# An input projection of 88 column tiles: 60 of them as 30 pairs of seven block products, with weight sums formed on the chip

## The chip, the cores and the metric

The kernel runs on one core of a Trainium2 chip. The metric is the device time of one execution in microseconds (us), the median of repeated runs. Engines are named as the profile names them: PE is TensorE's matmul and PEld its weight load, DVE is VectorE, ACT is ScalarE, POOL is GpSimd, SP is SyncE, which here issues most of the loads.

## What is computed

One layer of a hybrid backbone over 640 tokens (128 of context, 512 latent) of width 2048. Only its front matters here: a modulation vector from the conditioning, a normalised and modulated input `h`, and the combined input projection of 11,312 columns.

```python
mod = (cond @ p['w_mod'][l] + p['b_mod'][l])[:, None, :]
shift1, scale1, gate1, shift2, scale2, gate2 = jnp.split(mod, N_MOD, axis=-1)
h = rmsnorm(x, p['pre1_gain'][l]) * (1 + scale1) + shift1
...
proj = h @ p['w_in'][l] + p['b_in'][l]
(dq, dk, dv, dz, db, da, mq, mk, mv, mo, mi, mf, ga, gb) = split_columns(proj)
```

Two recurrent branches, their merge, and sixteen experts follow; the change doesn't touch them. All values are float32.

## The kernel before

All of the front is in `phase_front` (L163). The projection is cut into 88 column tiles of 128 columns and a gate tile of 48 (tile number 88). The result of a tile is 128 channels by 640 tokens, in two PSUM banks of 320 tokens each (`CHUNKS`), and it sums over 16 slices of 128 inputs. For float32 accuracy, each operand is split into a rounded high part and a low rest, and a product is taken as high x high + high x low + low x high. So a tile is 16 x 3 x 2 = 96 matmuls of 320 columns, in `products` (L288), called by `project` (L303).

The stages of a tile run on different engines. SP loads its weights (1 MB, from `d_win`) into a ring of four slots (L231 to L239). ACT makes the high half (`high`, L410), DVE the low half (`low`, L539), each two tiles ahead, and PE waits for `win_low`. After the matmuls ACT evicts the two banks with the bias (L476 to L486), and POOL stores the 320 KB of the tile (L255). Tiles 0 to 23 get a convolution instead, on DVE and ACT; tiles 24 to 39 are evicted in column-major token order; tiles 40 to 87 as they are.

Between the tiles runs the modulation product: 96 chunks of 128 inputs (1 MB each, from `d_wmod`), four matmuls of 512 columns each, in the four column strips of the array, so that they run side by side (`mod_products`, L265; the compiler makes two passes of each). Chunks 0 to 31 come before the projection; of the other 64 one comes before each tile from 24 on. Sixteen chunks are a group, which sums in one bank. At its end ACT copies the sums out (`copy_mod`, L393), PE turns them (`turn_mod`, L275), and DVE adds the bias (`store_mod`, L514). ACT issues the copy behind the last but one tile of a group (L489), and PE has a whole tile to do before it needs it.

The order of the loads is fixed by `mod_place` and `win_place` (L153 to L160). PE's program has loops over tiles 1 to 16 and over tiles 24 to 87 (L345); the programs of the other engines are written out. Behind the gate tile PE turns the gates (L361 to L366), DVE copies them, and the phase ends.

## Time and profile before

| | |
|---|---|
| median of 3 runs | 3760.63 us (3759.98 to 3760.92) |
| the profiled execution | 3755.26 us, of which the span from first to last instruction is 3753.4 us |
| PE busy | 3444.1 us, 92% of the span |
| DVE busy | 1960.6 us, 52% |
| ACT busy | 1663.3 us, 44% |
| POOL busy | 305.3 us, 8% |
| mean granted clock of TensorE | 0.959 of full speed |
| matmuls of L292 (the projection) | 8544, the first at 110.7 us, the last at 1466.9 us |

Matmuls are pipelined: the duration of one matmul in the trace is longer than its distance to the next one, so costs are taken from distances of starts. The idle time of an engine that waits for the one that is the bound costs nothing. "Granted clock" is the share of full speed that the chip allows TensorE; a mean of a stretch lies between its two levels, 0.5 (1.2 GHz) and 1.0 (2.4 GHz).

### The profile page before, as it was taken

The numbers are of one execution on the slowest core, as the hardware profiler recorded it, in microseconds if no ns is written. First come the engines' busy times: TensorE is split into PE (matmuls) and PEld (weight loads), VectorE is DVE, ScalarE is ACT, GpSimd is POOL, SyncE is SP. The second block draws the span as 40 slices with busy tenths as digits, with TensorE's granted clock in tenths as the row PEclk, the third lists the DMA queues.
The fourth block names the chain that finished last, engine by engine and source line by source line (L and its number), as shares of the span: only waits on it lengthen the run. The fifth ranks groups of instructions, "written<-read, shape, count | busy, mean of one in ns | idle before, by whom it ended". The sixth has DMA issues, their size and how long they took to land. (4 is left out here: it accounts for less than half of the span.)

```text
span 3753.4 us, 49971 instructions
## 1 busy us (share of the span) xinstructions
PE 3444.1 (92%) x20467; PEld 2846.4 (76%) x20467; DVE 1960.6 (52%) x2072; ACT 1663.3 (44%) x2033; POOL 305.3 (8%) x320
## 2 busy tenths in 40 slices
PE   5999999999999996999774899995999999999994
PEld 0899999999999996898753898875666666666663
DVE  1577411111111111545568434265888888888886
ACT  2445222211111112555432323343777777777774
POOL 0000000000000001332200100000001001010001
PEclk8999999999999998999986999996999999999997
DMA  9322344444444442112132533375999999999997
GB/s 410 135 91 89 107 157 156 159 157 161 158 166 162 156 156 80 48 34 67 42 91 68 194 121 127 134 292 223 360 399 385 391 399 376 400 391 382 398 378 293
DMA packets 172483, 796.85 MB, mean 212 GB/s; under 512 B 16532, under 2 KB 74132, under 8 KB 85284
## 3 DMA queue, kind: packets, MB, share of 16 engines
q1 hardware_dynamic: 154132, 701.71, 49.2%
q0 software_dynamic: 17328, 87.63, 7.0%
q10 hardware_dynamic: 864, 5.27, 0.3%
q8 instruction: 114, 1.87, 0.2%
q14 instruction: 45, 0.37, 0.0%
HBM read 732.10 MB, written 62.46 MB: 212 GB/s over the span
## 5 line engine op out<-in xcount | busy, mean ns | idle before, releaser
L2071 DVE TENSOR_TENSOR expert_lo<-expert_ring,expert_hi 128x2048 fp32r<-128x2048 f32 x384 | 879.4, 2291 | 159.6 <-ACT expert_hi L2008 156.5
L2008 ACT ACTIVATE expert_hi<-expert_ring 128x2048 fp32r<-128x2048 f32 x384 | 735.8, 1917 | 251.7 <-PE bank L1955 228.9
L292 PE MATMUL bank<-h_hi,win_hi 128*128 128x320 f32 x2848 | 656.1, 311 | 0.0
L292 PE MATMUL bank<-h_lo,win_hi 128*128 128x320 f32 x2848 | 647.1, 308 | 0.0
L292 PE MATMUL bank<-h_hi,win_lo 128*128 128x320 f32 x2848 | 646.9, 308 | 0.0
L541 DVE TENSOR_TENSOR win_lo<-front_ring,win_hi 128x2048 fp32r<-128x2048 f32 x89 | 203.8, 2290 | 821.3 <-ACT win_hi L414 821.3
L292 PEld LDWEIGHTS bank<-h_hi,win_hi 128*128 128x128 f32 x2848 | 473.1, 188 | 55.3 <-issue 55.3
L292 PEld LDWEIGHTS bank<-h_lo,win_hi 128*128 128x128 f32 x2848 | 476.4, 188 | 0.0
L292 PEld LDWEIGHTS bank<-h_hi,win_lo 128*128 128x128 f32 x2848 | 476.3, 188 | 0.0
L1953 PE MATMUL bank<-expert_hi,xeT_hi 128*80 128x512 f32 x1024 | 404.0, 395 | 1.2 <-DVE xeT_lo L2076 1.2
L1954 PE MATMUL bank<-expert_lo,xeT_hi 128*80 128x512 f32 x1024 | 402.3, 393 | 0.0
L1955 PE MATMUL bank<-expert_hi,xeT_lo 128*80 128x512 f32 x1024 | 398.9, 390 | 0.0
L485 ACT ACTIVATE x_tok<-bank,chan 128x320 f32<-128x320 f32 x96 | 45.3, 523 | 598.4 <-PE bank L292 598.4
L1576 ACT ACTIVATE merge_w_hi<-merge_ring 128x2048 fp32r<-128x2048 f32 x48 | 92.0, 1916 | 308.3 <-PE bank L1502 161.2
L1955 PEld LDWEIGHTS bank<-expert_hi,xeT_lo 128*80 128x80 f32 x1024 | 151.8, 148 | 85.8 <-issue 0.7
L1953 PEld LDWEIGHTS bank<-expert_hi,xeT_hi 128*80 128x80 f32 x1024 | 151.4, 148 | 84.8 <-issue 2.2
L1954 PEld LDWEIGHTS bank<-expert_lo,xeT_hi 128*80 128x80 f32 x1024 | 151.6, 148 | 81.0 <-issue 0.7
L1953 PE MATMUL bank<-expert_hi,hiddenT_hi 128*80 128x512 f32 x512 | 204.1, 399 | 0.0
L1954 PE MATMUL bank<-expert_lo,hiddenT_hi 128*80 128x512 f32 x512 | 200.9, 392 | 0.0
L1955 PE MATMUL bank<-expert_hi,hiddenT_lo 128*80 128x512 f32 x512 | 200.3, 391 | 0.0
L1668 DVE TENSOR_TENSOR merge_w_lo<-merge_ring,merge_w_hi 128x2048 fp32r<-128x2048 f32 x48 | 110.0, 2292 | 127.2 <-ACT merge_w_hi L1576 125.8
L414 ACT ACTIVATE win_hi<-front_ring 128x2048 fp32r<-128x2048 f32 x89 | 171.2, 1924 | 2.6 <-DMA front_ring<-d_win 2.6
(336 smaller groups left out, 4701.4 us busy)
## 6 DMA issues: line engine op xcount, KB each, us to landing
expert_ring<-d_wgate SPq DMA_DIRECT2D x128, 1024.0 KB, 7.2
expert_ring<-d_wup_e SPq DMA_DIRECT2D x128, 1024.0 KB, 7.8
expert_ring<-d_wdown SPq DMA_DIRECT2D x128, 1024.0 KB, 10.4
front_ring<-d_wmod SPq DMA_DIRECT2D x96, 1024.0 KB, 7.1
front_ring<-d_win SPq DMA_DIRECT2D x89, 1024.0 KB, 4.9
merge_ring<-d_wout SPq DMA_DIRECT2D x32, 1024.0 KB, 5.0
d_proj<-x_tok POOLq DMA_DIRECT2D x88, 320.0 KB, 2.5
merge_ring<-d_wup SPq DMA_DIRECT2D x16, 1024.0 KB, 5.0
```

Of the source, the lines that this page charges most:

```text
L292: mm = pe.matmul(bank[b][c][:, 0:hi - lo], wt[:, kk, :], h[:, kk, lo:hi], start=(kk == 0 and wt is w_hi[b] and h is k.h_hi), stop=(kk == K ...
L414: act.activation(w_hi[n % 2][:].rearrange("p k n -> p (k n)"), ring[place % FRONT_SLOTS][:], ACT.Copy).then_inc(s["win_high"], 1)
L485: ev = act.activation(ob[b][:, lo:hi], bank[b][c][:, 0:hi - lo], ACT.Identity, bias=bias(n))
L541: dve.tensor_tensor(w_lo[n % 2][:].rearrange("p k n -> p (k n)"), ring[win_place(n) % FRONT_SLOTS][:], w_hi[n % 2][:].rearrange("p k n -> ...
L1576: act.activation(w_hi[n % 2][:], w[:, n % 2], ACT.Copy).then_inc(s["w_high"], 1)
L1668: dve.tensor_tensor(w_lo[n % 2][:], w[:, n % 2], w_hi[n % 2][:].bitcast(F32), ALU.subtract).then_inc(s["w_low"], 1)
L1953: pe.matmul(out[0:CAP, :], a_hi, hi, start=first, stop=False)
L1954: pe.matmul(out[0:CAP, :], a_hi, lo, start=False, stop=False)
L1955: return pe.matmul(out[0:CAP, :], a_lo, hi, start=False, stop=last)
L2008: act.activation(w_hi[n % NSPLIT][:], w[:, n % NSLOT].rearrange("p (k n) -> p k n", n=HALF), ACT.Copy).then_inc(s["we_high"], 1)
L2071: dve.tensor_tensor(w_lo[n % NSPLIT][:], w[:, n % NSLOT].rearrange("p (k n) -> p k n", n=HALF), w_hi[n % NSPLIT][:].bitcast(F32), ALU.subt ...
```

## The change

Tiles 28 to 87 are taken in 30 pairs. A pair's weights are a 2 x 2 grid of blocks: the tile (first or second of the pair) by the half of the inputs (eight slices of 128). The tokens are a 2 x 2 grid too: half of the tokens (320) by half of the inputs. In place of the eight block products of the two tiles, seven are taken (Strassen's form with Winograd's order of sums), named by their weights: B11, T3, T1, T2, B21, T4, B22. T1 to T4 are sums of weight blocks, made by DVE for every pair. S1 to S4 are sums of the token blocks, made by DVE once (S1 to S3 during tiles 26 to 28, S4 in pair 0). Every sum is split into high and low halves like a plain operand. A block product is 8 x 3 = 24 matmuls of 320 columns into one bank. ACT and DVE put the products together into the four output blocks.

The order is now: tiles 0 to 23, the gate tile, tiles 24 to 27 (29 "classic" tiles in all), then the pairs. The modulation chunks 32 to 35 come at the classic places 21 to 24; the last 60 come as 120 halves of 512 KB through one buffer (`mod_half`), four per pair: after B11, T1, B21 and B22. Weights of the pairs come in quarters of 512 KB, each reloaded as soon as its product is done. High halves have three slots. `copy_mod` of a group comes in the pair after its last half, behind that pair's B11. PE's second loop is gone. The gates are turned behind tile 24 (the classic place 25); the vectors of the modulation are turned at the end. `h` and its halves keep their size but are laid out by token half.

The diff, cut to its core, in the order SP, PE, ACT, DVE, data layout (inner lines are moved to the left; output branches for the column-major tiles are left out):

```diff
+    def load_part(p, j, sem):
+        tile, half = PAIR_TILE + 2 * p + (j in (T3, B22)), (j in (B21, B22))
+        sp.dma_start(part(p, j)[:], k.d_win[tile][:, HALF_K * half:HALF_K * (half + 1), :]
+                     ).then_inc(s[sem], 16)
+    def load_mod_half(u):
+        if u < 4 * N_PAIRS:
+            wait(sp, s["half_used"], u)
+            q, h = half_of(u)
+            sp.dma_start(mod_half[:], k.d_wmod[q][:, 1024 * h:1024 * (h + 1)]).then_inc(s["half_in"], 16)
...
+    sp.wait_ge(s["s_low"], 3)
+    load_part(0, B21, "b21_in")
+    sp.wait_ge(s["proj_summed"], N_CLASSIC)
+    load_mod_half(0)
+    for p in range(N_PAIRS):
+        for j, sem in ((B11, "b11_in"), (T3, "b12_in"), (T1, "b22_in"), (B21, "b21_in")):
+            if p + 1 < N_PAIRS:
+                sp.wait_ge(s["part_summed"], part_number(p, j) + 1)
+                load_part(p + 1, B22 if j == T1 else j, sem)
+            if j != T3:
+                load_mod_half(4 * p + 1 + (B11, T1, B21).index(j))
+        load_mod_half(4 * p + 4)
 @block.gpsimd
...
+    def mod_half_chunk(u):
+        q, h = half_of(u)
+        g, kk = divmod(q, KT)
+        pe.wait_ge(s["half_in"], 16 * (u + 1))
+        if kk == 0 and h == 0:
+            pe.wait_ge(s["mod_copied"], g)
+        for j in range(4):
+            mm = pe.matmul(mod_sum(g)[32 * j:32 * j + 2, 256 * h:256 * (h + 1)], cond[:, kk, :],
+                           mod_half[:, 256 * j:256 * (j + 1)], start=(kk == 0 and h == 0),
+                           stop=(kk == KT - 1 and h == 1))
+        mm.then_inc(s["half_used"], 1)
...
+    def part_products(p, j):
+        m = part_number(p, j)
+        pe.wait_ge(s["part_low"], m + 1)
+        hi, lo = part_hi[m % HI_SLOTS], part_lo(p, j)
+        left_hi, left_lo = left[j]
+        for kk in range(HALF_K):
+            for x, (w, a) in enumerate(((hi[:, kk, :], left_hi), (hi[:, kk, :], left_lo),
+                                        (lo[:, kk, :], left_hi))):
+                mm = pe.matmul(part_bank[j][:, 0:HALF_T], w, a[:, kk, :],
+                               start=(kk == 0 and x == 0),
+                               stop=(kk == HALF_K - 1 and x == 2))
+        mm.then_inc(s["part_summed"], 1)
...
+    for p in range(N_PAIRS):
+        if p == 0:
+            pe.wait_ge(s["evac"], N_CLASSIC + 1)
...
+            pe.wait_ge(s["out_made"], MADE * p - 2)
+        part_products(p, B11)
+        mod_half_chunk(4 * p)
+        if p == 0:
...
+        else:
+            pe.wait_ge(s["out_made"], MADE * p - 1)
+        part_products(p, T3)
+        if p == 0:
...
+        else:
+            pe.wait_ge(s["out_made"], MADE * p)
+        part_products(p, T1)
+        mod_half_chunk(4 * p + 1)
+        part_products(p, T2)
...
+            turn_mod(GROUP_END[p - 1])
+        pe.wait_ge(s["p1_copied"], p + 1)
+        part_products(p, B21)
+        mod_half_chunk(4 * p + 2)
+        pe.wait_ge(s["out_made"], MADE * p + 2)
+        part_products(p, T4)
...
+            pe.wait_ge(s["s_low"], 4)
+        part_products(p, B22)
...
     def copy_mod(g):
-        act.wait_ge(s["mod_used"], KT * (g + 1))
+        if g < 2:
+            act.wait_ge(s["mod_used"], KT * (g + 1))
+        else:
+            act.wait_ge(s["half_used"], last_half(g))
...
+    def part_high(p, j):
+        m = part_number(p, j)
+        if m >= HI_SLOTS:
+            act.wait_ge(s["part_summed"], m - HI_SLOTS + 1)
+        if j in (B11, B21, B22):
+            act.wait_ge(s[{B11: "b11_in", B21: "b21_in", B22: "b22_in"}[j]], 16 * (p + 1))
+        else:
+            act.wait_ge(s["t_sum"], 4 * p + 1 + (T1, T3, T2, T4).index(j))
+        act.activation(part_hi[m % HI_SLOTS][:], part(p, j)[:], ACT.Copy).then_inc(s["part_high"], 1)
...
+    for p in range(N_PAIRS):
+        na = PAIR_TILE + 2 * p
+        act.wait_ge(s["part_summed"], part_number(p, B11) + 1)
+        wait(act, s["out_made"], MADE * p)
+        act.activation(u2[:], bank_a[:, 0:HALF_T], ACT.Copy)
+        wait_store(act, na)
+        if na < T_MLQ + PERM_TILES:
...
+        else:
+            act.activation(ob[0][:, 0:HALF_T], bank_a[:, 0:HALF_T], ACT.Identity, bias=bias(na)
...
+        for j in range(7):
+            m = part_number(p, j) + HI_SLOTS
+            if m < 7 * N_PAIRS:
+                part_high(*divmod(m, 7))
...
+            if j == B11 and p - 1 in GROUP_END:
+                copy_mod(GROUP_END[p - 1])
+    copy_mod(MOD_GROUPS - 1)
     act.wait_ge(s["rowp_in"], 16)
...
+    def t_sum(p, j):
+        out = part(p, j)[:]
+        if j == T1:
+            dve.wait_ge(s["b12_in"], 16 * (p + 1))
+            dve.wait_ge(s["b11_in"], 16 * (p + 1))
+            combine(out, b12[:], b11[:], ALU.subtract).then_inc(s["t_sum"], 1)
...
+    def split_low(m):
+        if m < 7 * N_PAIRS:
+            dve.wait_ge(s["part_high"], m + 1)
+            dve.tensor_tensor(part_lo(*divmod(m, 7))[:], part(*divmod(m, 7))[:],
+                              full(part_hi[m % HI_SLOTS][:]), ALU.subtract
+                              ).then_inc(s["part_low"], 1)
...
+    low(T_MLQ + 2)
+    dve.wait_ge(s["gates_turned"], 1)
+    dve.tensor_copy(k.gates[:], k.bank[6][:, 0:TT * 48].rearrange("p (t n) -> p t n", t=TT)
+                    ).then_inc(s["gates_copied"], 1)
...
+    combine(s1, full(a_hi[1][0]), full(a_hi[1][1]), ALU.add)
+    combine(s1, s1, full(a_lo[1][0]), ALU.add)
+    combine(s1, s1, full(a_lo[1][1]), ALU.add).then_inc(s["s_sum"], 1)
+    combine(s2, s1, full(a_hi[0][0]), ALU.subtract)
+    combine(s2, s2, full(a_lo[0][0]), ALU.subtract).then_inc(s["s_sum"], 1)
+    low(T_MLQ + 3)
+    s_low(0, s1_lo[:], s1_hi[:], s1)
...
+    low(T_MLQ + 4)
+    s_low(1, s2_lo[:], s2_hi[:], s2)
...
+    s_low(2, s3_lo[:], s3_hi[:], s3_sum[:])
...
+    for j in (T1, T3, T2):
+        t_sum(0, j)
+    split_low(0)
+    split_low(1)
+    t_sum(0, T4)
+    split_low(2)
...
+        split_low(part_number(p, B11) + HI_SLOTS)
+        if p == 0:
+            combine(s4_sum, full(a_hi[0][1]), full(s2_hi[:]), ALU.subtract)
+        split_low(part_number(p, T3) + HI_SLOTS)
+        if p == 0:
+            combine(s4_sum, s4_sum, full(s2_lo[:]), ALU.subtract)
+            combine(s4_sum, s4_sum, full(a_lo[0][1]), ALU.add).then_inc(s["s_sum"], 1)
+        split_low(part_number(p, T1) + HI_SLOTS)
+        dve.wait_ge(s["part_summed"], part_number(p, T2) + 1)
+        dve.wait_ge(s["p1_copied"], p + 1)
+        dve.tensor_tensor(u2[:], u2[:], bank_b[:, 0:HALF_T], ALU.add)
+        dve.drain().then_inc(s["out_made"], 1)
+        dve.tensor_tensor(u3[:], u2[:], bank_c[:, 0:HALF_T], ALU.add)
+        dve.drain().then_inc(s["out_made"], 1)
...
+        dve.drain()
+        dve.tensor_tensor(u2[:], u2[:], bank_d[:, 0:HALF_T], ALU.add)
+        dve.drain().then_inc(s["out_made"], 1)
+        if nxt:
+            t_sum(p + 1, T1)
+            t_sum(p + 1, T3)
+        if p == 0:
+            s_low(3, s4_lo, s4_hi, s4_sum)
+        split_low(part_number(p, T2) + HI_SLOTS)
+        if p - 1 in GROUP_END:
+            store_mod(GROUP_END[p - 1])
+        dve.wait_ge(s["part_summed"], part_number(p, B21) + 1)
...
+        else:
+            made = dve.tensor_tensor(ob[0][:, 0:HALF_T], ob[0][:, 0:HALF_T], bank_a[:, 0:HALF_T], ALU.add)
+        made.then_inc(s["out_made"], 1)
+        split_low(part_number(p, B21) + HI_SLOTS)
+        dve.wait_ge(s["part_summed"], part_number(p, T4) + 1)
...
+        else:
+            made = add_out(ob[0][:, HALF_T:T], bank_c[:, 0:HALF_T], bias(na), u3[:])
+        made.then_inc(s["out_made"], 1)
+        if nxt:
+            t_sum(p + 1, T2)
+        split_low(part_number(p, T4) + HI_SLOTS)
+        dve.wait_ge(s["part_summed"], part_number(p, B22) + 1)
+        if turned:
...
+        else:
+            made = add_out(ob[1][:, 0:HALF_T], bank_d[:, 0:HALF_T], bias(nb), u2[:])
+        made.then_inc(s["out_made"], 1)
+        if nxt:
+            t_sum(p + 1, T4)
+        split_low(part_number(p, B22) + HI_SLOTS)
     store_mod(MOD_GROUPS - 1)
...
-    whole = w.reshape(KT, P, MOD_GROUPS, D)[:, :, 2:].transpose(2, 0, 1, 3)
+    whole = w.reshape(KT, P, MOD_GROUPS, 4, 2, 256)[:, :, 2:].transpose(2, 0, 1, 4, 3, 5)
```

## Rows read from the trace of the kernel before

**Rows 1.** busy in one stretch: us, PE, PEld, DVE, ACT, POOL; clock, DMA share, GB/s

```profile
471.74:1467.28 995.54, 991.57 (x6769) 924.24 (x6761) 151.93 (x80) 193.68 (x228) 35.10 (x65) 1.00 0.40 153
```

**Rows 2.** timeline, ACT: start, us, engine, line, op; tiles 22, 23, 86, 87, gate

```profile
457.29 0.37 ACT L421 ACTIVATE x_tok<-bank,chan 128x128 f32<-128x128 f32 x1 [7.62 <-PE bank L292]
...
471.37 0.37 ACT L421 ACTIVATE x_tok<-bank,chan 128x128 f32<-128x128 f32 x1 [7.60 <-PE bank L292]
...
1437.52 0.94 ACT L485 ACTIVATE x_tok<-bank,chan 128x320 f32<-128x320 f32 x2 [12.51 <-PE bank L292]
...
1452.77 0.95 ACT L485 ACTIVATE x_tok<-bank,chan 128x320 f32<-128x320 f32 x2 [10.24 <-PE bank L292]
...
1467.28 0.36 ACT L493 ACTIVATE x_tok<-bank,chan 48x128 f32<-48x128 f32 x1 [13.57 <-PE bank L292]
```

**Rows 3.** timeline, PE, two matmuls in the expert stage

```profile
2622.89 0.39 PE L1953 MATMUL bank<-expert_hi,xeT_hi 128*80 128x512 f32 x1
2623.12 0.39 PE L1954 MATMUL bank<-expert_lo,xeT_hi 128*80 128x512 f32 x1
```

**Rows 4.** groups of instructions, 800 to 1400 us: busy, mean ns, idle before

```profile
L541 DVE TENSOR_TENSOR win_lo<-front_ring,win_hi 128x2048 fp32r<-128x2048 f32 x39 | 89.4, 2292 | 508.8 <-ACT win_hi L414 508.8
L414 ACT ACTIVATE win_hi<-front_ring 128x2048 fp32r<-128x2048 f32 x39 | 74.5, 1911 | 0.0
L267 PE MATMUL bank<-front_ring,cond 128*2 128x512 f32 x312 | 40.6, 592 | 2.6 <-issue 2.6
L485 ACT ACTIVATE x_tok<-bank,chan 128x320 f32<-128x320 f32 x78 | 36.8, 523 | 486.7 <-PE bank L292 486.7
...
L397 ACT ACTIVATE mod_rows<-bank 2x512 f32<-2x512 f32 x8 | 4.7, 586 | 0.1
...
L277 PE MATMUL bank<-const,mod_rows 128*128 128x128 f32 x8 | 1.2, 272 | 0.0
```

**Rows 5.** the same view, 130 to 370 us, one group of VectorE

```profile
L563 DVE TENSOR_TENSOR x_tok<-x_tok 128x640 f32<-128x640 f32 x16 | 13.1, 818 | 0.0
```

**Rows 6.** timeline, PE, one modulation chunk between two tiles

```profile
778.05 1.04 PE L267 MATMUL bank<-front_ring,cond 128*2 128x512 f32 x8
```

**Rows 7.** DMA, 800 to 1400 us: a queue; issues, KB each, median us to landing

```profile
q8 instruction: 36, 0.59, 0.4%
...
front_ring<-d_win SPq DMA_DIRECT2D x39, 1024.0 KB, 4.9
front_ring<-d_wmod SPq DMA_DIRECT2D x39, 1024.0 KB, 7.0
d_proj<-x_tok POOLq DMA_DIRECT2D x39, 320.0 KB, 2.4
```

**Rows 8.** the same view at 1841 us, one load

```profile
Cs<-d_smc SPq DMA_DIRECT2D x1, 512.0 KB, 3.8
```

**Rows 9.** timeline, PE, merge stage: four waits, idle time in brackets

```profile
2305.89 0.77 PE L1522 MATMUL bank<-merge_w_hi,yA_hi 128*128 128x512 f32 x1 [3.43 <-DVE yA_lo L1673]
...
2457.72 0.50 PE L1522 MATMUL bank<-merge_w_hi,yB_hi 128*128 128x512 f32 x1 [1.93 <-DVE merge_w_lo L1668]
...
2500.89 0.50 PE L1522 MATMUL bank<-merge_w_hi,yB_hi 128*128 128x512 f32 x1 [3.19 <-DVE merge_w_lo L1668]
...
2532.06 0.50 PE L1522 MATMUL bank<-merge_w_hi,yB_hi 128*128 128x512 f32 x1 [3.68 <-DVE merge_w_lo L1668]
```

**Rows 10.** PE by stretch, the microseconds behind those waits: busy, clock, DMA

```profile
2305.89:2313.89 8.00, 8.00 (x23) 0.64 0.90 346
2457.72:2465.72 8.00, 8.00 (x28) 0.79 0.95 356
2500.89:2508.89 8.00, 8.00 (x35) 1.00 0.63 204
2532.06:2539.00 6.94, 6.94 (x23) 0.75 0.49 151
```

**Rows 11.** timeline, DVE, the last instruction of the stage

```profile
1470.16 0.41 DVE L614 COPY gates<-bank 128x240 f32<-128x240 f32 x1 [2.48 <-PE bank L364]
```

More of the change, by code:

```diff
@@ L150, with tile_of, front_loads, part_number @@
 N_MOD_LOADS = MOD_GROUPS * KT
-def mod_place(q):
-    return q if q < 28 else q + 2 if q < 2 * KT else 58 + 2 * (q - 2 * KT)
-def win_place(n):
-    return 28 + n if n < 2 else 32 + n if n < T_MLQ + 2 else 59 + 2 * (n - T_MLQ - 2)
+HALF_T, HALF_K = T // 2, KT // 2
+N_CLASSIC = 29
+PAIR_TILE = 28
+N_PAIRS = (N_TILES - PAIR_TILE) // 2
+EARLY_MODS = 2 * KT + 4
+B11, T3, T1, T2, B21, T4, B22 = range(7)
+HI_SLOTS = 3
+MADE = 7
+def tile_of(o):
+    return o if o < T_MLQ else GATE_TILE if o == T_MLQ else o - 1
+def front_loads():
+    loads = [("mod", q) for q in range(28)] + [("win", o) for o in range(2)]
+    loads += [("mod", q) for q in range(28, 2 * KT)]
+    for o in range(2, N_CLASSIC):
+        if 23 <= o < 27:
+            loads.append(("mod", 2 * KT + o - 23))
+        loads.append(("win", o))
+    return loads
+FRONT_LOADS = front_loads()
+FRONT_PLACE = {load: place for place, load in enumerate(FRONT_LOADS)}
+def part_number(p, j):
+    return 7 * p + j
 def phase_front(nc, k):
+    def overlay(stack, specs):
+        return [stack.enter_context(nc.sbuf_tensor(n, shape, dt)) for n, shape, dt in specs]
+    QUARTER = [P, HALF_K, P]
+    TOKENS = [P, HALF_K, HALF_T]
     with ExitStack() as mem:
@@ new lines, in phase_front @@
+        with ExitStack() as between:
+            overlay(between, [("s3_front", [P, D], F32)])
+            s3_sum, = overlay(between, [("s3_sum", TOKENS, F32)])
+        PARTS = ("x0", "x1", "x2", "x3", "b21", "b12", "b11")
+        with ExitStack() as between:
+            sums = overlay(between, [(f"part_{n}", QUARTER, F32) for n in PARTS])
+        lows = overlay(mem, [(f"part_lo_{n}", QUARTER, F32R) for n in PARTS])
+        s3_lo, s3_hi = overlay(mem, [(n, TOKENS, F32R) for n in ("s3_lo", "s3_hi")])
@@ new lines, in phase_front @@
+        ob = overlay(mem, [(f"out_rows{b}", [P, T], F32) for b in range(2)])
+        w_hi, w_lo = (w_hi0, w_hi1), (w_lo0, w_lo1)
+        a_hi, a_lo = ([[h[:, r, HALF_K * c:HALF_K * (c + 1), :] for c in range(2)] for r in range(2)]
+                      for h in (k.h_hi, k.h_lo))
+        s4_hi, s4_lo = a_hi[1][0], a_lo[1][0]
+        s4_sum = k.h_lo_sum[:, 1, 0:HALF_K, :]
+        left = {B11: (a_hi[0][0], a_lo[0][0]), T3: (s3_hi[:], s3_lo[:]), T1: (s1_hi[:], s1_lo[:]),
+                T2: (s2_hi[:], s2_lo[:]), B21: (a_hi[0][1], a_lo[0][1]), T4: (a_hi[1][1], a_lo[1][1]),
+                B22: (s4_hi, s4_lo)}
@@ L179, in phase_front, with part_place, part, part_lo @@
+        place_of = {B22: 0, T1: 1, T2: 2, T4: 3}
+        def part_place(p, j):
+            return {B21: 4, T3: 5, B11: 6}[j] if j in (B21, T3, B11) else (place_of[j] + p) % 4
+        def part(p, j):
+            return sums[part_place(p, j)]
+        def part_lo(p, j):
+            return lows[part_place(p, j)]
+        b21, b12, b11 = sums[4:]
         RAW = T + 8
@@ L208, in phase_front @@
         x_sample, x_prompt = k.bank[4:6], k.bank[6:8]
-        N_PLAIN = N_TILES - T_MLQ
+        bank_a, bank_c, bank_d, bank_b = k.bank[2], k.bank[3], k.bank[0], k.bank[1]
+        part_bank = {B11: bank_a, T3: bank_c, T1: bank_d, T2: bank_b, B21: bank_a, T4: bank_c, B22: bank_d}
         def mod_sum(g):
```

279 lines of the change are left out of this document (190 added, 89 removed).

## The prediction

> **What bounds the kernel now.** I first read the busy time by stretch for the stage that the change touches, from the last tile of the convolved kind to the gate tile [rows 1]: TensorE is busy 991.57 of 995.54 us at a granted clock of 1.00, VectorE 151.93, ScalarE 193.68, and the DMA engines hold a share of 0.40. The stage ends when TensorE has issued its matmuls. The timeline of ScalarE then gives the cost of a tile, since its first eviction starts as the tile's last matmul ends [rows 2]. Tiles 22 to 23 are 471.37 - 457.29 = 14.08 us apart: 96 matmuls of 320 columns, 0.1467 us each. Tiles 86 to 87 are 15.25 apart: 1.17 us for one chunk of the modulation product between them. From tile 87 to the gate tile it is 14.51: 0.43 for four transposes. Tiles 17 to 23 are already written out without a loop, so straight-line code feeds TensorE at this pace; in the stage's loop 36 instruction fetches stand in 600 us [rows 7]. Of the stage, from 471.37 to the last gates copy at 1470.57 [rows 2, 11], 999.2 us are to be compared.
>
> **Taken away.** Sixty tiles were 60 x 8 half-by-half block products of 24 matmuls for 30 pairs of 16; now each pair has 7 block products over all 24 matmuls of 320 columns, where it had 8. A block is 24 x 0.1467 = 3.52 us, so a pair takes 24.64 where its two tiles took 28.16, and 30 pairs save 105.6 us. Both operand shapes stay. New is that 24 matmuls in a row add into one bank, where two banks took turns. In the expert stage three in a row add into one bank at 0.22 to 0.23 us for 512 columns [rows 3]: 0.213 of that is streaming at 2.4 GHz, the rest 0.01 to 0.02. The 320 columns stream in 0.133 of 0.1467, the same rest, so I take no loss.
>
> **The modulation chunks.** Of 96 chunks 60 now come as 120 halves, each a 512 KB load and 256 columns per matmul. A chunk's eight matmuls start in two waves of four: 1.04 us in all, 592 ns each [rows 4, 6]. A matmul of this type takes 592 ns at 512 columns and 272 at 128, so 0.833 ns per column and 379 at 256. Two waves each lose 0.213: 1.17 - 0.43 = 0.74 per half. Bounds are 0.585 (half a chunk) and 1.17 (no less than a whole). 120 x 0.74 = 88.8 against 60 x 1.17 = 70.2: a loss of 18.6. The four early chunks issued as 16 pieces stay at 1.17 each; if their halves serialise this adds up to 8 us, which I leave to the range.
>
> **New work beside TensorE.** Per pair VectorE gets eleven passes of 1024 elements and seven of 320. From 818 ns at 640 and 2292 at 2048 elements [rows 4, 5] they are 1.22 and 0.49 us: 13.4 + 3.4, with drains some 17.5 us in a pair of 27.6. ScalarE gets seven conversions of 1.1 (from 1911 at 2048) and two copies of 0.52: 8.7. Neither is the bound. What could bite is the order. Walking one steady pair from its first matmul: B11 ends at 3.5, T3 7.8, T1 11.3, T2 15.6, B21 19.1, T4 23.3, B22 26.9. The tightest step is the low half of B22: VectorE can start its four output sums at 15.6, then two weight sums, then this subtraction, ending at 21.8; TensorE wants it at 23.3. A third weight buffer and 7 us between release and use cover the others by 3 us and more. If VectorE took 25% longer, B22 would be the late one.
>
> **One-time waits.** Before tile 27's products VectorE has, from the gates' transposes on, a copy, five sums of 2560 elements (2.85 each) and then the 2.29 us split: 17 us, while TensorE has one tile of 14.08: 3.2 us idle. At the first pair the conversion is queued behind the last tile's eviction in three pieces (an estimate of 1.3, from 0.52 for 320 columns): 1.3 + 1.1 + 1.22, with handovers 3.7 us idle. In pair 0 three more sums of 2.85 and a subtraction stand ahead of B22: 3.4 us. Sum 10.3.
>
> **The copy at a group's end.** At pairs 6, 14 and 22 the half chunk behind B11 opens a new group and waits until ScalarE has copied the old one out. ScalarE gets there only after B11: copies 0.52 + 0.52, a conversion 1.1, then four copies of 0.586: with handovers 4.6 us, in which all of T3 to B22 is queued behind on TensorE. Before, this copy ran behind a whole tile. 3 x 4.6 = 13.8.
>
> **The load with the least cover.** There is one buffer for halves. Three of a pair's four loads have two blocks, 7.0 us; the one issued after B22's half is wanted after B11 alone, 3.52 us later, with SP free. Durations on SP are 4.9 us for 1 MB with the next megabyte 2.5 behind it (7.0 + 0.37 - 4.9), and 2.4 for a 320 KB store [rows 7]; the one undisturbed 512 KB load took 3.8 [rows 8]. Interpolating the first two gives 3.1, halving the megabyte 3.7. I take 3.8, the row of its own size: 3.8 + 0.1 - 3.52 = 0.4 us per pair, 26 pairs (the other three are under the copy): 10.4. Bounds: 0 at 3.1; 1.2 if the 320 KB store of the pair's second tile, issued in the same moment, goes first (0.31 of a megabyte, 0.77 us).
> The Trainium skill (DMA: Bandwidth & Descriptors, section Anatomy of one DMA) fits a load as about 2.0 us plus its bytes at 436 GB/s, an estimate of 3.2 us here; by it these 10.4 us would be 0. By the same fit a megabyte takes 4.4, where [rows 7] show 4.9, so the measured size decides.
>
> **The clock.** In the merge stage, TensorE stood idle 3.43, 1.93, 3.19 and 3.68 us after dense work [rows 9], and in the 8 us behind the mean clock was 0.64, 0.79, 1.00 and 0.75 [rows 10]: three of four times it fell from 2.4 to 1.2 GHz for some microseconds, worth 2.9, 1.7, 0 and 1.7 us of full speed. Six waits above are 3.2 us or longer; at the mean 1.6 they cost 9.6 (0 to 17).
>
> **The tail.** The last group's copy and the vectors now lie behind the last block: the copy's 2.4, four transposes, some ten small VectorE operations, a transpose and a last copy. The small ones together I take at 3.0, an estimate from 0.41 for 240 columns [rows 11] and 0.43 for four transposes: 5.4 to VectorE's end. Before, the gates' tail was 3.3, and it moved under tile 25.
>
> **Sum from tile 23's end.** Five whole tiles 70.4, four early chunks 4.7, gates 0.5, blocks 739.2, halves 88.8, three turns 1.3, one-time 10.3, copies 13.8, load 10.4, clock 9.6, tail 5.4: 954.4. Against 999.2 that is 44.8 less. The profiled execution of 3755.26 would become 3710.5; the median of the runs, 3760.63, lies 5.4 higher, so 3716.
>
> **The rivals.** R1, all cover holds: load 0 and no clock loss, 20 less: 3696. For it the 3.1 and the 3.19 us idle without a fall; against, the row of 3.8. R2, the store goes first: 1.2 in place of 0.4, 29 x 0.77 = 22 more: 3738. For it is that both leave in the same half microsecond; against, that the load may be ahead.
> The Trainium skill (DMA: Bandwidth & Descriptors, section Queues, rings and completion order) says that a DMA engine takes turns between the rings that have work, packet by packet; by that rule R2 is what happens, and no row here has two such transfers overlapping.
> R3, a half chunk costs as much as a whole: 120 x 0.43 = 52 more: 3768, no gain. Against is the slope from 128 to 512 columns. R4, slower: the load behind B22 takes 5.3 us or longer, TensorE idles 1.9 us in every pair, and the clock falls each time as after the 1.93 us idle: 29 x (1.5 + 1.7) = 93 more: 3809. It decides from 5.3 us; against it stands that even a megabyte is in after 4.9. R5, the change doesn't do what it says: a block of one bank runs 10% slower: 74 more, 3790; against, [rows 3].
>
> **How the numbers follow.** Forecast 0.50, R1 0.20, R2 0.14, R3 0.05, R4 0.07, R5 0.04. About 0.2% (7.5 us) can be told from no change. Faster: the first three, 0.84; same 0.05 (most of R3); slower 0.11. The range goes from below R1 by half of the halves' lower bound (120 x 0.155 / 2 = 9), 3686, to above R2 by the early chunks and half the clock's bound (8 + 4), 3750.
>
> **What would show it.** Right: blocks 3.52 us apart; a half chunk adding 0.74; 27.6 to 28.1 us per steady pair; TensorE waiting for ScalarE's copy about 4.6 us in pairs 6, 14 and 22 with the clock at 0.5 behind; waits of 3 to 4 us before tile 27, pair 0 and B22 of pair 0. Wrong: waits of TensorE for weight sums or low halves in every pair (VectorE the bound), a wait for the half's load above 1.5 us, a mean clock well under 1 across the pairs, or blocks longer than 3.52.

## The result, and the profile after

| | before | after |
|---|---|---|
| median of the runs | 3760.78 us (3759.98 to 3762.13, 4 runs) | 3716.64 us (3714.08 to 3721.14, 4 runs) |
| profiled execution, its span | 3755.26, 3753.4 | 3714.25, 3712.5 |
| PE, DVE, ACT busy | 92%, 52%, 44% | 91%, 64%, 47% |
| mean granted clock | 0.959 | 0.953 |

The ratio is 0.9885, with a 95% interval of 0.9872 to 0.9898. The forecast was 3716. That the total came out so close is partly luck: single terms of the sum are off by several microseconds, and what the load cost differs by 5 us between two profiles of the same kernel. The profiles show where.

First the busy time by stretch of the kernel after (us, PE, PEld, DVE, ACT, POOL; clock, DMA share, GB/s): the whole stage from tile 23's end, pairs 1 to 5, pair 6, pairs 7 to 13, pair 14. [rows 1] is the same view of before.

```profile
473.04:1419.43 946.39, 914.60 (x6518) 834.48 (x6512) 561.76 (x589) 281.53 (x322) 35.16 (x65) 0.99 0.46 158
592.01:730.03 138.02, 137.98 (x1000) 125.27 (x992) 87.93 (x100) 42.22 (x50) 5.41 (x10) 1.00 0.50 177
730.03:765.03 35.00, 30.75 (x204) 27.76 (x204) 16.82 (x19) 10.39 (x14) 1.08 (x2) 0.90 0.41 137
765.03:959.91 194.88, 193.65 (x1400) 175.56 (x1400) 116.41 (x126) 57.13 (x63) 7.57 (x14) 1.00 0.51 175
959.91:994.37 34.46, 30.23 (x207) 27.25 (x211) 16.81 (x19) 10.39 (x14) 1.08 (x2) 0.90 0.42 143
```

Pairs 1 to 5 take 138.02 us, 27.6 each, and TensorE is busy in 137.98 of them. VectorE is busy 87.93 / 5 = 17.6 us of a pair and ScalarE 8.4. In pairs 6 and 14 TensorE stands idle 4.2 us and the clock is 0.90. ScalarE's timeline gives the borders, as in [rows 2]: the evictions at the classic places 25 to 28, then the copy that starts each pair's output (start, us, what it waited for). The gate tile stands at place 24, so these four are tiles 24 to 27; "tile 27" and "tile 28" below, as in the prediction, are the ones at places 27 and 28.

```profile
502.39 0.37 ACT L692 ACTIVATE out_rows<-bank,chan 128x128 f32<-128x128 f32 x1 [9.68 <-PE bank L438]
517.11 0.37 ACT L692 ACTIVATE out_rows<-bank,chan 128x128 f32<-128x128 f32 x1 [2.93 <-PE bank L438]
534.47 0.37 ACT L692 ACTIVATE out_rows<-bank,chan 128x128 f32<-128x128 f32 x1 [11.96 <-PE bank L438]
548.55 0.37 ACT L692 ACTIVATE out_rows<-bank,chan 128x128 f32<-128x128 f32 x1 [10.32 <-PE bank L438]
...
557.59 0.44 ACT L708 ACTIVATE u<-bank 128x320 f32<-128x320 f32 x1 [4.85 <-PE bank L473]
592.01 0.44 ACT L708 ACTIVATE u<-bank 128x320 f32<-128x320 f32 x1 [3.20 <-PE bank L473]
619.60 0.44 ACT L708 ACTIVATE u<-bank 128x320 f32<-128x320 f32 x1 [3.21 <-PE bank L473]
647.20 0.44 ACT L708 ACTIVATE u<-bank 128x320 f32<-128x320 f32 x1 [3.21 <-PE bank L473]
```

Tile 28 takes 14.08 us, a whole tile as before. Tile 27 takes 17.36, pair 0 34.42, and pairs 1 and 2 27.59 and 27.60. What TensorE waited for in this stage (us in total, times, longest):

```profile
PE bank L412 <- ACT mod_rows L584: 12.7, 3, 4.2
PE bank L473 <- DVE part_lo_x L858: 4.5, 1, 4.5
PE bank L473 <- DVE part_lo_b L858: 3.7, 1, 3.7
PE bank L438 <- DVE win_lo L767: 3.0, 1, 3.0
PE bank L412 <- DMA mod_half<-d_wmod: 3.0, 9, 0.6
PE bank L422 <- ACT mod_rows L584: 2.5, 1, 2.5
PE bank L549 <- DVEq L969: 1.1, 1, 1.1
```

These are the forecast's waits by place, one line each: the group's copy (three pairs), the low half of B22 in pair 0, the start of pair 0, tile 27, the load of the half, and two in the tail. The 8 us behind the three copies ran at these clocks (columns as above), which answers to [rows 10]:

```profile
734.40:742.40 8.00, 8.00 (x42) 7.20 (x35) 0.07 (x1) 1.06 (x1) 0.00 (x0) 0.64 0.21 70
964.30:972.30 8.00, 8.00 (x46) 7.22 (x39) 0.62 (x1) 1.06 (x1) 0.00 (x0) 0.72 0.26 83
1193.60:1201.60 8.00, 8.00 (x49) 7.64 (x42) 1.20 (x1) 1.06 (x1) 0.00 (x0) 0.79 0.33 111
```

In pair 2 (619.60 to 647.20) VectorE's steps between T2's end and the low half of B22 were:

```profile
631.63 0.49 DVE L913 TENSOR_TENSOR u<-u,bank 128x320 f32<-128x320 f32 x1 [1.94 <-PE bank L473]
...
634.47 1.22 DVE L832 TENSOR_TENSOR part_x<-part_b 128x1024 f32<-128x1024 f32 x1 [0.19 <-issue]
635.81 1.23 DVE L832 TENSOR_TENSOR part_b<-part_x,part_b 128x1024 f32<-128x1024 f32 x1
637.15 1.23 DVE L858 TENSOR_TENSOR part_lo_x<-part_x,part_hi 128x1024 fp32r<-128x1024 f32 x1
```

The low half is done at 638.38; B22 ends at 642.93 (where ScalarE's next conversion starts), so it began 3.52 us earlier, at 639.4. The tightest step has 1.0 us to spare.

### The profile page after: what moved, and what is told of

It reads as the page before. It is cut to its first block and busy times, and to the rows that moved or that the text cites. A ratio compares the mean times of both kernels' runs of the same rounds, so it can differ in the third digit from the quotient of the medians.

```text
span 3712.5 us, 50766 instructions
## 1 busy us (share of the span) xinstructions
PE 3377.8 (91%) x20259; PEld 2765.2 (74%) x20259; DVE 2370.4 (64%) x2579; ACT 1750.1 (47%) x2121; POOL 305.3 (8%) x320
## 5 line engine op out<-in xcount | busy, mean ns | idle before, releaser
L473 PE MATMUL bank<-h_hi,part_hi 128*128 128x320 f32 x960 | 304.8, 317 | 8.2 <-DVE part_lo_x L858 4.5
L473 PE MATMUL bank<-h_lo,part_hi 128*128 128x320 f32 x960 | 298.0, 310 | 0.0
L858 DVE TENSOR_TENSOR part_lo_x<-part_x,part_hi 128x1024 fp32r<-128x1024 f32 x120 | 147.1, 1226 | 164.9 <-ACT part_hi L686 157.8
L686 ACT ACTIVATE part_hi<-part_x 128x1024 fp32r<-128x1024 f32 x120 | 127.4, 1062 | 244.3 <-PE bank L473 244.3
L473 PE MATMUL bank<-s_hi,part_hi 128*128 128x320 f32 x720 | 231.2, 321 | 0.0
L473 PE MATMUL bank<-s_lo,part_hi 128*128 128x320 f32 x720 | 224.7, 312 | 0.0
L438 PE MATMUL bank<-h_hi,win_hi 128*128 128x320 f32 x928 | 214.7, 313 | 3.0 <-DVE win_lo L767 3.0
L438 PE MATMUL bank<-h_lo,win_hi 128*128 128x320 f32 x928 | 211.9, 310 | 0.0
L438 PE MATMUL bank<-h_hi,win_lo 128*128 128x320 f32 x928 | 211.7, 309 | 0.0
L473 PEld LDWEIGHTS bank<-h_hi,part_hi 128*128 128x128 f32 x960 | 181.5, 189 | 34.5 <-issue 34.5
```

The costliest lines, as they stand in the source:

```text
L438: mm = pe.matmul(bank[b][c][:, 0:HALF_T], wt[:, kk, :], h[:, c, kk, :], start=(kk == 0 and wt is hi and h is k.h_hi), stop=(kk == KT - 1 a ...
L473: mm = pe.matmul(part_bank[j][:, 0:HALF_T], w, a[:, kk, :], start=(kk == 0 and x == 0), stop=(kk == HALF_K - 1 and x == 2))
L686: act.activation(part_hi[m % HI_SLOTS][:], part(p, j)[:], ACT.Copy).then_inc(s["part_high"], 1)
L858: dve.tensor_tensor(part_lo(*divmod(m, 7))[:], part(*divmod(m, 7))[:], full(part_hi[m % HI_SLOTS][:]), ALU.subtract).then_inc(s["part_low" ...
```

## The experiments

All are edits of the kernel after, unless said otherwise. The length of a pair is the distance of two such starts as above. The experiments were timed on other occasions than the first table, with the kernel before beside them (median 3756.39 us for the first three sections, 3763.31 for the next three), so the ratios say more than differences from the kernel after, which are uncertain by some microseconds.

### The copy of a finished group, one pair earlier

```diff
-                        if j == B11 and p - 1 in GROUP_END:
-                            copy_mod(GROUP_END[p - 1])
+                    if p in GROUP_END and p + 1 < N_PAIRS:
+                        copy_mod(GROUP_END[p])
```

The new lines stand behind the loop over j, so ScalarE copies before it waits for the next pair's B11.

> ScalarE copies a finished modulation group out at the end of the pair that finishes it (behind the conversion of the next pair's T1), not one pair later behind B11. Theory: the 4.2 us wait of TensorE in pairs 6, 14 and 22 and the clock loss behind it (1.7 to 2.8 us by the lengths of the pairs) go away, since conversion 1.1 + copy 2.35 end 3.6 us after B22, and the half chunk that needs the bank comes 4.26 after it. These pairs, now 35.00, 34.46 and 33.90 us long, become 28.0 (27.6 + 0.43 for the transposes): 19.3 us less, about 3697. Rival: a wait of the same length is due there anyway (the half's load or the bank behind the transposes is late next): no gain, 3717. Between the two, if the clock falls without the wait: 12.6 less, 3704.

Measured: 3698.00 us (3694.72 to 3700.39, 4 runs), 0.9839 of the kernel before (0.9822 to 0.9855), 18.6 below the kernel after. Its list of TensorE's waits has no line for `mod_rows` in the pairs any more:

```profile
PE bank L473 <- DVE part_lo_x L858: 4.5, 1, 4.5
PE bank L412 <- DMA mod_half<-d_wmod: 3.8, 9, 1.0
PE bank L473 <- DVE part_lo_b L858: 3.7, 1, 3.7
PE bank L438 <- DVE win_lo L767: 3.0, 1, 3.0
```

Pairs 6, 14 and 22 took 28.03, 28.22 and 28.18 in place of 35.00, 34.46 and 33.90. So one copy cost 4.24 us of waiting and 2.7, 2.0 and 1.5 us of clock. Nothing else was late next.

### Two more passes on VectorE ahead of B22's low half

```diff
                     if nxt:
+                        dve.wait_ge(s["b12_in"], 16 * (p + 2))
+                        dve.wait_ge(s["b11_in"], 16 * (p + 2))
+                        for _ in range(2):
+                            combine(part(p + 1, T1)[:], b12[:], b11[:], ALU.subtract)
                         t_sum(p + 1, T1)
```

> VectorE makes the weight sum T1 of the next pair three times instead of once (two more passes of 1024 elements, 1.35 us each from start to start), ahead of the low half of B22. Theory: this low half is the tightest step of a pair; it ended 1.1 us ahead of TensorE's need (638.30 against 639.4 in the pair from 619.6), so with 2.7 more it is 1.6 us late in each of 29 pairs: 46 us, about 3763, and pairs of 29.2 us; if the clock falls at each of these waits too, up to 1.5 us more per pair, 3806. Rival: VectorE, idle for 10 of 27.6 us, takes it up: pairs stay 27.6 to 27.8, 3717.

Measured: 3768.43 us (3760.66 to 3781.82, 8 runs), 1.0034 of before (1.0021 to 1.0047): the whole gain is gone. From pair 1 on:

```profile
PE bank L473 <- DVE part_lo_x L858: 44.7, 28, 1.9
```

That is 1.6 us in each pair, as worked out from 2.7 us against a slack of 1.1, though VectorE is still idle for nearly a third of the pair. (The wait is 1.8 us in pairs 1 to 5, 1.5 or 1.9 in the later ones, and 1.1 in those with a group's copy.) Of the 25 pairs without a group's copy (and without pair 0), 20 took 29.4 to 29.7 us, so the wait alone, and five took 30.6 to 31.4. In three of these (pairs 2, 4 and 5) the clock fell, to 0.95 in the mean of the pair; in pairs 9 and 16 it stayed at 1.00, and TensorE waited 1.5 and 1.1 us more for the half's load. The first bound of the expectation was right, with little of the second.

### An eighth block product

```diff
                     pe.wait_ge(s["part_low"], m + 1)
+                    if j == T2:
+                        eighth(p)
...
+                    for kk in range(HALF_K):
+                        for x, (w, a) in enumerate(((hi[:, kk, :], left_hi), (hi[:, kk, :], left_lo),
+                                                    (lo[:, kk, :], left_hi))):
+                            pe.matmul(k.bank[5][:, 0:HALF_T], w, a[:, kk, :],
+                                      start=(kk == 0 and x == 0), stop=(kk == HALF_K - 1 and x == 2))
```

> One more block product of 24 matmuls in each pair, into a bank that nothing reads, ahead of T2 with T2's operands: as many matmuls as the kernel before, with the pairs' order, halves and sums kept. Theory: TensorE is the bound throughout the pairs, a block costs 3.52 us, and all else that the change adds is what is left: 105.6 more, 3822 (61 above the kernel before). Rival: something else sets the pair (VectorE's order, the loads), so part of the eighth block is hidden in waits of today: well under 105.6, pairs of less than 31.1 us.

Measured: 3823.78 us (3822.67 and 3824.90), 1.0176 of before (1.0156 to 1.0197), 107.1 above the kernel after. Pairs 1 and 2 took 31.12 and 31.11, 27.59 + 3.52. So a block that is left out is worth its full length, and all the rest of the change costs about 66 us (the 1.0176 of before; 3823.8 - 3756.4, with the median beside it, is 67).

### The load of the half chunk behind B22: late, or left out

In the first kernel the load is issued behind B11's matmuls, one block later:

```diff
+                        if j == B11 and p > 0:
+                            sp.wait_ge(s["part_summed"], part_number(p, j) + 1)
+                            load_mod_half(4 * p)
                         if p + 1 < N_PAIRS:
...
-                    load_mod_half(4 * p + 4)
```

> The load of the half chunk behind B11 is issued when B11's matmuls are done instead of one block earlier, so that TensorE waits for the whole load in each of 29 pairs: the price of the fourth rival of the prediction (a load that is late in every pair), with a longer wait. The load alone takes about 3.2 us by its absence of waits in pairs 1 to 5. Theory: 29 waits of about 3.3 us, and behind most of them the clock falls and costs 1.6 us as the forecast took it from the merge stage: 29 x 4.9 = 142, about 3859, pairs of 32.5 us. Rival: the wait alone, 29 x 3.3 = 96, about 3812, pairs of 31.1 us.

Measured: 3838.68 us (3834.43 and 3842.92), 1.0204 of before (1.0180 to 1.0229), 122 above the kernel after. From pair 1 on:

```profile
PE bank L414 <- DMA mod_half<-d_wmod: 86.5, 26, 3.9
PE bank L414 <- ACT mod_rows L586: 12.7, 3, 4.2
```

So 26 waits of 3.3 us, not 29: in three pairs the copy covers the load, which the expectation forgot. The 25 other pairs behind pair 0 took 32.51 in the mean: 27.59, the wait of 3.33, and 1.6 us of clock. Four took 30.8 to 31.0, with no loss of clock; 21 lost more than a microsecond. 26 x 4.9 is 127, near the 122. So the fourth rival's mechanism is real: a late load costs its wait, and behind waits of 3.1 to 3.9 us mostly the clock too. Its price isn't shown: it had the clock fall behind each wait of 1.9 us, and in the experiment with VectorE it fell behind 3 of 25 waits of 1.5 to 1.9. Its condition, a load of 5.3 us, is met by no load behind B22 in the first profile of the kernel after (the longest took 4.3) and by two of them in the second.

This kernel also shows the load without the store of the pair's second tile, which leaves 3.4 us ahead of it and has landed when it starts: 27 of its 29 loads took 3.1 to 3.4 us.

In the second kernel the load isn't issued at all:

```diff
-                    if u < 4 * N_PAIRS:
+                    if u < 4 * N_PAIRS and (u == 0 or u % 4):
...
-                    pe.wait_ge(s["half_in"], 16 * (u + 1))
+                    pe.wait_ge(s["half_in"], 16 * (u + 1 - u // 4))
```

> The load behind B22 is left out (29 of the 120 halves; the product of these halves takes what lies in the buffer, so this kernel computes another modulation). Theory: pairs 7 to 28, now 27.66 to 28.30 us long, all become 27.6, which is 5 us in all, and nothing else moves: about 3711. Rival, the forecast's term: 0.4 us per pair, 10 us. Second rival: the excess of these pairs isn't the load's (VectorE's low halves, code loading): they stay as they are.

Measured: one time of 3705.61 us; what counts is the length of pairs: all of 7 to 28 but the copies' took 27.58 to 27.60. From pair 0's copy to pair 29's it took 827.56 us in place of 832.85, so the load cost 5.3 in all in the first profile of the kernel after, half of the forecast's term.

Why pairs from 7 on wait for it, and of pairs 1 to 5 only pair 4 (27.66), is seen in the DMA issues of the kernel after (KB, us from issue to landing), around the end of pair 2 and of pair 9:

```profile
mod_half<-d_wmod SPq DMA_DIRECT2D x1, 512.0 KB, 3.0
d_proj<-out_rows POOLq DMA_DIRECT2D x1, 320.0 KB, 3.0
...
mod_half<-d_wmod SPq DMA_DIRECT2D x1, 512.0 KB, 3.7
d_proj<-out_rows POOLq DMA_DIRECT2D x1, 320.0 KB, 4.2
```

In pair 2 the load leaves at 643.50 and the store at 644.48; in pair 9 at 845.19 and 845.47. With the load left out, the same store landed after 2.4 us:

```profile
d_proj<-out_rows POOLq DMA_DIRECT2D x1, 320.0 KB, 2.4
```

So the two slow each other where they overlap: the load goes from 3.0 to 3.7 us, the store from 2.4 to 4.2. Of the 29 loads behind B22 of the kernel after, 25 go with the store's distance: 3.0 to 3.2 us where the store leaves 0.9 us or more later, 3.4 at 0.6, and 3.6 to 3.9 at 0.3, from pair 7 on. The cover is 3.5, and each of these later pairs is 0.2 us longer than 27.59.

The other four are those that pairs 4, 9, 21 and 26 wait for: 3.6, 4.2, 4.3 and 4.1 us. While they are under way, and while no other of the 29 is, a packet of the queue q8 starts, which fetches instructions. These pairs make up 2.0 of the 5.3 us. In the second profile of the kernel after, fetches fall on the same four loads, and they take 3.6, 6.2, 5.4 and 4.3 us. (There pair 6's load took 4.6 with no fetch starting in its time; the copy hides it.) The 6.2 (DMA from 816.5 to 823.5 us; packets, MB, share of 16 engines):

```profile
q8 instruction: 1, 0.02, 2.1%
...
mod_half<-d_wmod SPq DMA_DIRECT2D x1, 512.0 KB, 6.2
```

Behind it TensorE waited 2.6 us and pair 9 took 30.23; behind the 5.4 it waited 1.8, the clock fell, and pair 21 took 30.96. By the pairs' lengths above 27.59 the load cost 10.0 us in that profile, 6.9 of it in these four pairs. With the load left out the fetches slow the store instead: from pair 7 on it took 2.4 us in 18 of 22 cases, and 3.2, 3.0 and 3.1 ahead of pairs 9, 21 and 26. So the fetch is a second cause beside the store; it is read from what falls together in these profiles, and no kernel with the fetches moved was run.

### Order of VectorE's one-time work, and the copy at three places

Three changes in one kernel, each read at its own place. In VectorE's program:

```diff
                 combine(s1, s1, full(a_lo[1][1]), ALU.add).then_inc(s["s_sum"], 1)
+                low(T_MLQ + 3)
...
-                low(T_MLQ + 3)
                 s_low(0, s1_lo[:], s1_hi[:], s1)
+                low(T_MLQ + 4)
                 dve.wait_ge(s["mod_used"], EARLY_MODS)
...
-                low(T_MLQ + 4)
...
-                    split_low(part_number(p, B11) + HI_SLOTS)
                     if p == 0:
                         combine(s4_sum, full(a_hi[0][1]), full(s2_hi[:]), ALU.subtract)
+                    split_low(part_number(p, B11) + HI_SLOTS)
...
-                    if nxt:
+                    if nxt and p > 0:
                         t_sum(p + 1, T1)
                         t_sum(p + 1, T3)
...
                     split_low(part_number(p, T2) + HI_SLOTS)
+                    if p == 0:
+                        t_sum(p + 1, T1)
+                        t_sum(p + 1, T3)
```

In ScalarE's, `copy_mod` stands ahead of the copy to `u2` in pair 6, behind B11's conversion as it was in pair 14, and between the output copy and that conversion in pair 22.

> Three places of the changed kernel, each to be read by itself in the trace. (1) VectorE makes the low halves of tiles 27 and 28 ahead of the sums S2 and S3 instead of behind them: theory, the 3.0 us wait before tile 27's products goes away; rival, VectorE's whole work there is too long and the wait comes back at tile 28 or at the first pair (there 3.7 us today). (2) In pair 0 the first sum of S4 is made while VectorE waits for the first converted weights, and the weight sums of pair 1 come behind the low half of B22: theory, TensorE's 4.5 us wait for that low half goes away, and pair 0, 34.42 us long, becomes about 30; rival, S4 itself is late (three sums, a conversion, a subtraction) and 2 us or more stay. (3) The copy of a modulation group: in pair 6 ahead of ScalarE's two output copies, in pair 14 as it was, in pair 22 between output copies and conversion; waits of 4.2 us today should become 2.6, 4.2 and 3.1. If the clock falls only behind longer waits, pair 6 is 27.6 + 0.4 + 2.6 = 30.6 long; if it falls behind any, 32 and more. Whole kernel about 3 + 4 + 3 us below the changed kernel, too little to be told from one time.

Measured: one time of 3704.46 us. The stage's waits of TensorE:

```profile
PE bank L412 <- ACT mod_rows L584: 10.1, 3, 4.2
PE bank L412 <- DMA mod_half<-d_wmod: 5.6, 11, 2.6
PE bank L473 <- DVE part_lo_b L862: 3.9, 2, 3.7
...
PE bank L473 <- DVE part_lo_x L862: 0.6, 1, 0.6
```

(1) The line of tile 27 is gone, and pair 0's first copy starts at 554.40 instead of 557.59. (2) The 4.5 us became 0.6, and pair 0 took 28.69 in place of 34.42: 3.9 of waiting and 1.8 more, its clock. (3) In pair 6 the wait is 2.6 us, and this time the clock stayed up in the 8 us from 727 on:

```profile
724.12 0.61 PE L412 MATMUL bank<-mod_half,cond 128*2 128x256 f32 x8 [2.57 <-ACT mod_rows L584]
```

```profile
727.00:735.00 8.00, 8.00 (x59) 7.37 (x59) 2.52 (x3) 2.12 (x2) 0.00 (x0) 1.00 0.47 155
```

Here the length of one pair misleads, since the copy also delays the start it is measured by; pairs 5 and 6 together took 58.27, which is 2 x 27.59, 0.43 for the transposes and 2.66. Pair 14 (wait 4.2) took 34.84, pair 22 (3.3) 34.01: there the clock fell.

### The gains together

The copy behind B22 and VectorE's orders (1) and (2) in one kernel.

> The copy of a group at the end of the pair that finishes it (as in the kernel with the copy behind B22) together with the orders of VectorE (1) and (2) of the kernel with the three places. Theory: the gains add, as all lie on TensorE's path at different times: 19 for the copies, 3 before tile 27, 4 in pair 0, and 1 to 2 of clock: about 3689. Rival: the waits before tile 27 and in pair 0 come back elsewhere, 3697.

Measured: 3689.05 us (3687.08 to 3691.97, 5 runs), 0.9808 of before (0.9793 to 0.9823), against 0.9885 for the change alone: 27.6 us below the kernel after. What is left of TensorE's waits in the stage, but for the tail's two lines:

```profile
PE bank L412 <- DMA mod_half<-d_wmod: 4.2, 11, 1.7
PE bank L473 <- DVE part_lo_b L858: 3.9, 2, 3.7
...
PE bank L473 <- DVE part_lo_x L858: 0.6, 1, 0.6
```

### Both kernels again: what the stages that nobody touched do

From the first pair of profiles, the projection stage gained more than the kernel: 51.1 us from VectorE's end to VectorE's end (1470.57 and 1419.43), but 40.9 in the span. Five more profiles were to say whether the rest of the kernel had become slower.

> The kernel before, unchanged, for a second profile of it. From the first to the changed kernel's profile the projection stage became 52.8 us shorter (999.2 to 946.4), but the whole span only 40.9; the DeltaNet stage behind it, whose code is the same, went from 354.9 to 361.4 us. Theory A: that is scatter from one execution to the next (clock falls at some of its waits and not at others); then this second profile has a DeltaNet stage that differs from 354.9 by some us. Theory B: the change causes it; then this profile has 354.9 within 1 us, and every kernel with the pairs has about 361.

> The kernel before, for a third profile. DeltaNet's stage took 355.2 and 355.0 us in its two profiles and 353.5 to 361.8, 357.8 in the mean, in the eight profiles of kernels with the pairs; the router 74.4 and 82.4 against 72.7 to 82.8. Theory A (scatter of the clock from execution to execution, whatever the kernel): some of three more profiles of before have a DeltaNet stage of 357 or more. Theory B (the change makes it longer, by some 3 us): all are at 355 within 1 us.

> The same as the third profile of the kernel before: DeltaNet at 357 us or more in some of them (scatter), or all at 355 within 1 us (the change's doing).

> The same as the third profile of the kernel before: DeltaNet at 357 us or more in some of them (scatter), or all at 355 within 1 us (the change's doing).

> The changed kernel, for a second profile: TensorE's waits in the projection stage are set by order and must come again at the same size (copies 3 x 4.2, pair 0 3.7 and 4.5, tile 27 3.0 us). What the clock costs behind the three copies, 2.7, 2.0 and 1.5 us in the first profile, is expected between 1 and 3 each; the load waits 3 us in all within 2.

Measured (us; gates' first matmul to the end of the span, and in it DeltaNet and the router, each from its first matmul to the first of the next stage):

| profile | to the end | DeltaNet | router |
|---|---|---|---|
| before, five | 2271.5, 2280.2, 2276.7, 2281.5, 2273.6 | 355.2, 355.0, 356.2, 356.6, 356.2 | 74.4, 82.4, 75.8, 82.3, 75.7 |
| after, two | 2278.9, 2278.7 | 359.0, 358.9 | 76.1, 76.1 |
| seven edits of after | 2270.2 to 2282.4 | 353.5 to 361.8 | 72.7 to 82.8 |

The five of before are 2276.7 in the mean, the nine with the pairs 2278.3, over the same spread. The first profile of before, on which the forecast stands, was the shortest of its five, 5 us below their mean. For DeltaNet alone neither theory's numbers came: no profile of before reached 357, but they are not within 1 us of 355 either, and kernels with the pairs go from 2 us below them to 5 above. The means are 355.8 and 357.9; whether those 2 us are the change's stays open. The total says that it isn't much. (The 354.9 and 361.4 of the first expectation are not what these marks give; by them the first two profiles have 355.2 and 359.0.)

The second profile of after showed the same waits to the tenth (12.7, 4.5, 3.7, 3.0), but more for the half's load than the 3 us within 2 that were expected:

```profile
PE bank L412 <- DMA mod_half<-d_wmod: 5.6, 6, 2.6
```

The two longest are those of pairs 9 and 21 told above. Pairs 6, 14 and 22 took 35.01, 35.11 and 34.90: by the same comparison 2.7, 2.7 and 2.5 us of clock, within the 1 to 3 expected. VectorE's last copy ends at 1426.44, 7.0 us later than in the first profile, and the span is 6.8 longer: the two executions differ in this stage, not behind it.

## Why the prediction was right, and where it wasn't

**Blocks and halves.** Right to the hundredth. Pairs 1 to 5 took 27.6 us, 7 x 3.52 + 4 x 0.74, with TensorE busy throughout; the eighth block cost 3.52 each. One bank for 24 matmuls is no loss, and a half chunk takes 0.74. R3 and R5 are out.

**VectorE's order.** The walk through a steady pair held: low half of B22 done 22.3 us after the pair's first matmul (forecast 21.8), needed at 23.3. The slack was 1.0 us (0.9 to 1.2 by the experiment's waits) in place of 1.5, so "25% longer" was too generous: two passes more, 2.7 us or 15%, were late in every pair.

**One-time waits.** Forecast 3.2, 3.7 and 3.4; measured 3.0, 3.7 and 4.5. The prediction gave the last without its working. The trace has the three sums and S4's low half (2.8 each), as it named them, and pair 1's two weight sums, which the steady walk has at this place too; where the other 1.1 us come from wasn't looked into. That this order is the cause is shown: with the first sum earlier and the weight sums later the wait was 0.6.

**The copy at a group's end.** Forecast 4.6 each, measured 4.2; the experiment took this wait away, and the clock's loss behind it.

**The load.** This step failed in its mechanism. The forecast took the row of its own size, 3.8 us [rows 8], as the time of an undisturbed load, and so had 0.4 us in each pair. With the store gone, or 0.9 us behind it, the load takes 3.0 to 3.4 and costs nothing; with the lower bound of 3.1 from [rows 7] the forecast would have said 0. The row was no like for like: its 512 KB move in packets of 1 KB (113 packets, 0.12 MB, from 1843.3 us on), the half's in packets of 4 KB (144 packets, 0.52 MB, from 643.45 us on, 16 of them tiny); whether that is the difference wasn't tried. What costs anything is what else is under way: the store, the mechanism of R2, and a fetch of instructions, which no rival of the prediction has. The store adds 0.7 us to the load, of which 0.5 is covered, where R2 had 0.77 with nothing covered: 0.2 us a pair, some 3.4 in all. The fetches cost 2.0 in the first profile and 6.9 in the second (with the store's share in their pairs). So the term of 10.4 measured 5.3 and 10.0, and the second is close by luck. R1 and R2 were each half right. One of the prediction's signs of being wrong, a wait for the half above 1.5 us, came twice in the second profile (2.6 and 1.8), in single pairs.

The Trainium skill (DMA: Bandwidth & Descriptors, section Anatomy of one DMA — SWDGE (gpsimd) path), from which the prediction worked out an estimate of 3.2 us, gives its fit for transfers that GpSimd issues, and this load is issued by SP; the 3.0 to 3.4 without the store agree with it all the same. The same page's section Queues, rings and completion order has a DMA engine take turns between rings that have work; the trace agrees as far as it goes: load and store both get longer, 3.0 to 3.7 and 2.4 to 4.2, and neither is held back until the other is done.

**The clock.** Forecast 9.6, a mean of 1.6 for six waits. Measured behind the copies 2.7, 2.0 and 1.5, in pair 0 2.3 (34.42 - 27.59 - 4.5) and 1.7 at its start (its B11 took 5.3 in place of 3.52), behind tile 27 0.3 (17.36 - 14.08 - 3.0): 10.5. The mean was right; single waits go from 0.3 to 2.7, and to 0 in other kernels.

**The sum.** From 473.04 on: five tiles 70.4, one early chunk 1.2, gates 0.5, blocks 739.2, halves 87.8 (119 of them; the last lies in the tail), turns 1.3, one-time waits 11.2, copies 12.7, load 5.3 (3.0 of it in the list of waits), clock 10.5, and 5.65 from the last block (1413.78) to VectorE's end: 945.8, against 946.39 measured. The three other early chunks lie ahead of 473.04; 3.5 us were forecast for them, but tile 23 ended only 1.7 later than before (1.6 later than the mean of the five profiles of before, 471.4). What gave the rest back there wasn't looked into.

**The tail.** Its length was about right (5.4 forecast; 4.9 without the last half chunk, 5.65 with it), but its end mark was wrong. In both kernels the next stage's first VectorE instruction starts 8.2 us after POOL's instruction that stores the vectors, not after VectorE's end:

```profile
1467.97 0.54 POOL L257 DMA_DIRECT2D d_rows<-vec_rows  x1 [13.43 <-DVE vec_rows L612]
...
1476.16 0.24 DVE L643 TENSOR_TENSOR gate_x<-gates,rowp 128x80 f32<-128x80 f32 x1 [5.59 <-PEq L222]
```

```profile
1419.73 0.54 POOL L374 DMA_DIRECT2D d_rows<-vec_rows  x1 [4.36 <-DVE vec_rows L971]
...
1427.91 0.24 DVE L1000 TENSOR_TENSOR gate_x<-gates,rowp 128x80 f32<-128x80 f32 x1 [8.48 <-PEq L306]
```

The first fence is of before: there the store left while the gates' tail was still running, which hid part of it. The change moved it behind everything: 2.9 us that the sum lacks. That the stage's end waits for this store is read from the equal distances (8.2 us in all fourteen profiles, of nine kernels); it wasn't tried by itself.

**The total.** The sum said 954.4 us from tile 23's end (471.37 before). The stage took 948.06 from there in the first profile, 6.3 better, and 955.07 in the second, 0.7 worse; most of these 7 us are the two long loads and the clock behind the copies. In both, 2.9 were lost to the store. The stages behind took some 2 us more than the mean of before's five profiles, which isn't told from their scatter. That the first profile of before was 5 us short there did no harm, since the forecast added 5.4 back on the way to the median. In the medians 44.1 us were gained, with an interval from 38 to 48, where 44.8 were forecast. So the sum is right within what can be told, but with terms off both ways that cancel: in the first profile the load (5 us too much) against the store (2.9 too little) and the stages behind.

## What to carry to other kernels

When a step leaves the bound engine with fewer instructions, walk one steady period and find the step with the least slack: here an engine idle for 10 of 27.6 us was 1 us away from eating the gain. Rare copies and first-time sums are set by their place in one engine's program, and moving a few lines was worth 27.6 us, well over half of the 44 that the change itself brought. For a transfer with little cover look at what else leaves in the same microsecond, stores and instruction fetches too, and check that the row its price comes from moves its bytes alike; for the end of a stage at the last store, not at the last computation.
